# Two stacked blocks of layers: the second block's layer norms rewritten, and all layer loops written out

## The reference, cut to what matters

```
def layer_norm(x, g, b):
    mu = mean(x); var = mean(square(x - mu))      # over the 1024 features of a token
    return (x - mu) * rsqrt(var + 1e-5) * g + b

def second_block(x, p, ...):
    for i in range(2):
        proj = x @ w_in[i]                        # attention, retention, gates
        ...
        y = merged @ w_out[i]
        x = layer_norm(ALPHA * x + y, ln1_g[i], ln1_b[i])
        ffn = conv_glu_ffn(x, w_up[i], conv_w[i], conv_b[i], w_down[i])
        ple = sigmoid(x @ w_ple_gate[i]) * (p[i] @ w_ple_proj[i])
        x = layer_norm(ALPHA * x + ffn + ple, ln2_g[i], ln2_b[i])
    return x
```

## Time and profile before

| What | Value |
|---|---|
| Median of three runs | 2084.21 us (2080.54 to 2084.79) |
| Profiled execution | 2079.78 us, span 2078.0 us |
| Mean granted TensorE clock | 0.987 |
| TensorE busy | 2020.5 us, 97% |
| VectorE, ScalarE, POOL busy | 63%, 52%, 15% |

### The profile page before, as it was taken

The page is one execution under the profiler, slowest core; times in us unless marked ns, Lnnn a source line. Parts: engine busy times, 40 slices in busy tenths (PEclk is TensorE's granted clock), DMA queues, the critical chain, the costliest instruction groups (busy, mean ns, idle before and its releaser), DMA issues.

```text
span 2078.0 us, 36494 instructions
## 1 busy us (share of the span) xinstructions
PE 2020.5 (97%) x14488; PEld 1890.8 (91%) x14488; DVE 1301.7 (63%) x1504; ACT 1086.8 (52%) x1312; POOL 320.1 (15%) x239
## 2 busy tenths in 40 slices
PE   6999999999999999999999999999998999999997
PEld 5999999899889999998999999999998999998996
DVE  6555666655665576567556655577775655557775
ACT  5444565544554455655446544356655553455654
POOL 3000431300020014033003012230004203220001
PEclk9999999999999999999999999999998999999998
DMA  6554544455445545445455544554453544544551
GB/s 248 189 188 171 181 146 163 161 187 188 169 172 188 186 164 182 158 168 197 182 184 185 179 145 160 184 197 182 182 182 123 185 161 146 185 167 169 200 186 42
DMA packets 53286, 360.04 MB, mean 173 GB/s; under 512 B 6320, under 2 KB 7728, under 8 KB 10544
## 3 DMA queue, kind: packets, MB, share of 16 engines
q1 hardware_dynamic: 49248, 350.01, 46.6%
q10 hardware_dynamic: 3328, 4.20, 0.7%
q0 software_dynamic: 592, 4.19, 0.5%
HBM read 353.14 MB, written 1.05 MB: 170 GB/s over the span
## 4 chain that ended last, share of the span: by engine, by line
PE 60%; issue 30%; POOL 5%; DVE 2%; ACT 2%; DMA 1%; SPq 0%; POOLq 0%; DVEq 0%; ACTq 0%
PE up_two L1392 7%; PE gate_two L1357 7%; PE gate_two L1392 7%; PE gate_two L1358 7%; PE gate_two L1359 7%; PE bank L1357 5%; PE bank L1359 5%; PE bank L1358 5%; PE up_two L1394 4%; PE gate_two L1394 3%; POOL br_parts L404 2%; POOL in_parts L404 1%; POOL area L443 1%; PE bank L1469 1%; ACT w_hi L544 1%
## 5 line engine op out<-in xcount | busy, mean ns | idle before, releaser
L920 DVE TENSOR_TENSOR w_lo<-raw,w_hi 128x2048 fp32r<-128x2048 f32 x330 | 765.2, 2320 | 331.1 <-ACT w_hi L544 330.9
L544 ACT ACTIVATE w_hi<-raw 128x2048 fp32r<-128x2048 f32 x330 | 628.4, 1905 | 72.7 <-PE bank L1359 68.7
L1358 PE MATMUL bank<-hid_hi,w_lo 128*128 128x256 f32 x960 | 271.6, 283 | 0.0
L1357 PE MATMUL bank<-hid_lo,w_hi 128*128 128x256 f32 x960 | 271.5, 283 | 0.0
L1359 PE MATMUL bank<-hid_hi,w_hi 128*128 128x256 f32 x960 | 271.5, 283 | 0.0
L1392 PE MATMUL gate_two<-in_parts,w_hi 128*128 128x512 f32 x640 | 229.1, 400 | 4.9 <-POOL in_parts L404 4.9
L1357 PE MATMUL gate_two<-br_parts,w_hi 128*128 128x256 f32 x768 | 222.9, 290 | 9.3 <-POOL br_parts L404 8.4
L1392 PE MATMUL up_two<-in_parts,w_hi 128*128 128x512 f32 x640 | 227.8, 398 | 0.4 <-DVE w_lo L920 0.4
L1359 PE MATMUL gate_two<-br_parts,w_hi 128*128 128x256 f32 x768 | 218.8, 285 | 0.0
L1358 PE MATMUL gate_two<-br_parts,w_lo 128*128 128x256 f32 x768 | 218.7, 285 | 0.0
L1357 PEld LDWEIGHTS bank<-hid_lo,w_hi 128*128 128x128 f32 x960 | 183.7, 191 | 3.0
(11 more groups left out here) (257 smaller groups left out, 4465.4 us busy)
## 6 DMA issues: line engine op xcount, KB each, us to landing
raw<-stream SPq DMA_DIRECT2D x330, 1024.0 KB, 4.8
area<-rpb POOLq DMA_DIRECT2D x2, 1536.0 KB, 7.0
softT<-area ACTq DMA_DIRECT2D x32, 64.0 KB, 4.4
konst<-consts SPq DMA_DIRECT2D x1, 1344.0 KB, 13.2
x<-xT SPq DMA_DIRECT2D x4, 256.0 KB, 3.8
area<-area ACTq DMA_DIRECT2D x8, 128.0 KB, 5.6
ret_turn<-area ACTq DMA_DIRECT2D x8, 128.0 KB, 2.3
result<-x SPq DMA_DIRECT2D x4, 256.0 KB, 2.0
```

What stands on the lines that cost most here:

```text
L544: act.activation(w_hi[:, s, :], raw[:, s, :], ACT.Copy).then_inc(hi_ready[s], 1)
L920: dve.tensor_tensor(w_lo[:, s, :], raw[:, s, :], w_hi[:, s, :].bitcast(F32), ALU.subtract).then_inc(lo_ready[s], 1)
L1357: pe.matmul(out, whi, xlo, start=start, stop=False, skip_group_check=True)
L1358: pe.matmul(out, wlo, xhi, start=False, stop=False, skip_group_check=True)
```

## The change

In the second block:
- The variance is summed by 8 products with mean_of as the fixed operand and the squares (128x256) moving, so that it comes out the same on all 128 partitions, 128x256 in PSUM (var_ln). ScalarE adds the epsilon on the way to SBUF (rstd_ln, 128x256), and POOL raises this whole tile to -0.5. The spreading product ln_factor is gone.
- Subtraction of the mean and squares go by pairs of tiles (128x512), 4 each.
- The pair sums move from POOL to VectorE, between its additions to x.
- The lower parts move from POOL to VectorE: work + bias - br_hi, one tile behind the scaling. ScalarE first writes all upper parts and then x (in the first norm after chunk 37's work).
- The last norm makes no upper and lower parts.
- In the first norm both engines split the slot of chunk 36 ahead of their part of the norm. At the end of layer 0 the split of slot CHUNKS-3 moves into that chunk's step, and the one of CHUNKS-2 ahead of the norm on VectorE.

In both blocks the loops over layers are Python loops, so each layer has its own instructions; gains and biases are read from col1 and col2, without copies. The FFN's inner loop stays. The core of the diff:

```diff
+        rstd_ln = sb("rstd_ln", [P, T])
-        rstd_ln = banks[7][:, 1, :]
+        var_ln = banks[7][:, 0, :]
 # POOL
             def layer_norm(here, n):
-                for j in (1, 2):
-                    pool.wait_ge(z_ready.sem, here.at(z_ready, HALVES * n + j + 1))
-                    if j == 2:
-                        pool.wait_ge(z_sum.sem, here.at(z_sum, 2 * n + 1))
-                    pool.tensor_tensor(z_pairs, x[:, 0:2, :] if j == 1 else z_pairs, x[:, 2 * j:2 * j + 2, :], ALU.add
-                                       ).then_inc(z_sum.sem, 1)
                 pool.wait_ge(ln_var.sem, here.at(ln_var, n + 1))
-                power(rs[:, :], ms[:, :]).then_inc(ln_rs.sem, 1)
-                for k in range(DT):
-                    pool.wait_ge(xs_hi.sem, here.at(xs_hi, DT * n + k + 1))
-                    rest(br_lo[:, k, :], x[:, k, :], br_hi[:, k, :]).then_inc(xs_ready.sem, 1)
+                pool.tensor_tensor(rstd_ln[:, :], rstd_ln[:, :], minus_half.broadcast_to([P, T]), ALU.pow
+                                   ).then_inc(ln_rstd.sem, 1)
-            with pool.Fori(0, DEPTH) as layer:
+            for layer in range(DEPTH):
 # ScalarE
-                def layer_norm(n, col_b, spare=lambda: None):
+                def variance(n):
                     act.wait_ge(var_ready.sem, here.at(var_ready, n + 1))
-                    act.activation(ms[:, :], banks[7][:, 0, 0:TT], ACT.Identity, bias=eps5).then_inc(ln_var.sem, 1)
-                    spare()
+                    act.activation(rstd_ln[:, :], var_ln, ACT.Identity, bias=eps5).then_inc(ln_var.sem, 1)
+
+                def shifted_upper(n, col_b):
+                    for k in range(DT):
+                        act.wait_ge(ln_scaled.sem, here.at(ln_scaled, DT * n + k + 1))
+                        act.activation(br_hi[:, k, :], work[:, k, :], ACT.Identity,
+                                       bias=cur[:, col_b + k:col_b + k + 1]).then_inc(xs_hi.sem, 1)
+
+                def shifted(n, col_b):
                     for k in range(DT):
                         act.wait_ge(ln_scaled.sem, here.at(ln_scaled, DT * n + k + 1))
                         act.activation(x[:, k, :], work[:, k, :], ACT.Identity, bias=cur[:, col_b + k:col_b + k + 1]
                                        ).then_inc(x_new.sem, 1)
-                        act.activation(br_hi[:, k, :], work[:, k, :], ACT.Identity, ...
...
                     elif m == 36:
-                        layer_norm(0, C_B1, ple_first)
+                        split_after(here, m)
+                        for a in range(2):
+                            e = act.activation(ple_out[:, 2 * a:2 * a + 2, :], banks[4 + a][:, :, :], ACT.Copy)
+                        e.then_inc(mix_evac.sem, 1)
+                        variance(0)
+                        shifted_upper(0, C_B1)
                     elif m == 37:
...
                         split_after(here, m)
+                        shifted(0, C_B1)
...
                         if c == CHUNKS[1] - 3:
+                            if layer < DEPTH - 1:
+                                split_after(here, c, turn)
                             hidden_upper(here, PAIRS - 1, att_hi)
...
                 centred_squares(1)
-                layer_norm(1, C_B2)
+                variance(1)
+                if layer < DEPTH - 1:
+                    shifted_upper(1, C_B2)
+                shifted(1, C_B2)
 # VectorE
                 def centred(n):
                     dve.wait_ge(mu_ready.sem, here.at(mu_ready, n + 1))
-                    for k in range(DT):
-                        dve.tensor_tensor(x[:, k, :], x[:, k, :], banks[6][:, 0, :], ALU.subtract).then_inc(c_ready.sem, 1)
+                    mu = banks[6][:, 0:1, :].broadcast_to([P, 2, T])
+                    for j in range(HALVES):
+                        two = x[:, 2 * j:2 * j + 2, :]
+                        dve.tensor_tensor(two, two, mu, ALU.subtract).then_inc(c_ready.sem, 1)
...
+                    def shifted_lower(k):
+                        dve.wait_ge(xs_hi.sem, here.at(xs_hi, DT * n + k + 1))
+                        dve.scalar_tensor_tensor(out=br_lo[:, k, :], in0=work[:, k, :],
+                                                 scalar=cur[:, col_b + k:col_b + k + 1],
+                                                 in1=br_hi[:, k, :].bitcast(F32), op0=ALU.add, op1=ALU.subtract
+                                                 ).then_inc(xs_ready.sem, 1)
                     dve.wait_ge(ln_rstd.sem, here.at(ln_rstd, n + 1))
                     for k in range(DT):
                         dve.scalar_tensor_tensor(out=work[:, k, :], in0=x[:, k, :], scalar=cur[:, col + k:col + k + 1],
-                                                 in1=rstd_ln, op0=ALU.mult, op1=ALU.mult).then_inc(ln_scaled.sem, 1)
+                                                 in1=rstd_ln[:, :], op0=ALU.mult, op1=ALU.mult
+                                                 ).then_inc(ln_scaled.sem, 1)
+                        if lower and k >= 1:
+                            shifted_lower(k - 1)
+                    if lower:
+                        shifted_lower(DT - 1)
...
                     elif m == 36:
-                        layer_norm(0, C_G1)
                         split_after(here, m)
+                        layer_norm(0, C_G1, C_B1)
...
                 centred(1)
-                with dve.If(layer < DEPTH - 1):
-                    chunk_done(here, CHUNKS[1] - 3)
-                    split_after(here, CHUNKS[1] - 3)
-                layer_norm(1, C_G2)
-                with dve.If(layer < DEPTH - 1):
+                if layer < DEPTH - 1:
                     chunk_done(here, CHUNKS[1] - 2)
                     split_after(here, CHUNKS[1] - 2)
+                layer_norm(1, C_G2, C_B2, layer < DEPTH - 1)
 # TensorE
                 def variance(n):
                     for f in range(DT):
-                        pe.wait_ge(c_sq.sem, here.at(c_sq, DT * n + f + 1))
-                        for a in range(TT):
-                            e = pe.matmul(banks[7][:, 0, a:a + 1], work[:, f, a * P:(a + 1) * P], mean_of[:, 0:1],
-                                          start=f == 0 and a == 0, stop=f == DT - 1, skip_group_check=True)
+                        pe.wait_ge(c_sq.sem, here.at(c_sq, HALVES * n + f // 2 + 1))
+                        e = pe.matmul(var_ln, mean_of, work[:, f, :], start=f == 0, stop=f == DT - 1)
                     e.then_inc(var_ready.sem, 1)
-                def ln_factor(n):
-                    pe.wait_ge(ln_rs.sem, here.at(ln_rs, n + 1))
-                    spread_factor(rstd_ln).then_inc(ln_rstd.sem, 1)
```

More of the change, by code:

```diff
@@ L499, in _ @@
             load_tables(0, 1)
-            with pool.Fori(0, DEPTH) as layer:
+            for layer in range(DEPTH):
                 here = Place(1, layer)
+                cur = col2[:, layer, :]
                 pool.wait_ge(xs_ready.sem, here.at(xs_ready, 0))
-                pool.wait_ge(cur_ready.sem, here.at(cur_ready, 1))
+                pool.wait_ge(decay_step, 3)
                 for h in range(RET_HEADS):
@@ L532, in _ @@
                 layer_norm(here, 0)
-                with pool.If(layer < DEPTH - 1):
-                    following = nc.s_assert_within(layer + 1, 1, DEPTH - 1, skip_runtime_bounds_check_because="the If bounds it")
-                    load_tables(following, layer + 2)
+                if layer < DEPTH - 1:
+                    load_tables(layer + 1, layer + 2)
                 layer_norm(here, 1)
@@ L667, in _ @@
             act.wait_ge(small_set, SMALL)
-            with act.Fori(0, DEPTH) as layer:
+            for layer in range(DEPTH):
                 here = Place(0, layer)
+                cur = col1[:, layer, :]
                 split_hi(2, here.uses(2))
@@ L754, in _ @@
                 ffn(here, FFN_CHUNKS + MIX1, 1)
-                norm_input(here, 3, gain1, range(HALVES))
+                norm_input(here, 3, gain1(layer + 1), range(HALVES))
             act.wait_ge(col2_in, 16)
@@ L901, in step @@
                         hidden_upper(here, i + 1)
[L902 to L906, removed]
+                    if c == CHUNKS[1] - 3:
+                        pass
+                    elif c == CHUNKS[1] - 2:
+                        if layer < DEPTH - 1:
+                            chunk_done(here, c, turn)
                             split_after(here, c, turn)
@@ L1075, in _ @@
                 dve.sem_inc(x_ready.sem, 1)
-                xg_lower(Place(0, 0), 0, gain1, [j])
+                xg_lower(Place(0, 0), 0, gain1(0), [j])
             for s in range(2):
                 split_lo(s, 0)
-            with dve.Fori(0, DEPTH) as layer:
+            for layer in range(DEPTH):
                 here = Place(0, layer)
-                dve.tensor_copy(cur[:, 0:COLS1], col1[:, bass.ds(layer, 1), :].rearrange("p a c -> p (a c)")
-                                ).then_inc(cur_ready.sem, 1)
```

(11 more changed lines are left out.)

58 lines of the change are left out of this document (30 added, 28 removed).

## The result

The changed kernel takes 2225.92 us (median of 4 runs, 2221.74 to 2229.66) against 2083.05 us for the kernel before beside it: a ratio of 1.0686 (1.0658 to 1.0715), slower by 143 us. The profiled execution took 2221.74 us.

A forecast was written before the change was run, and what follows sets the result against it. TensorE, busy 97% of the span, was taken as the bound, so exposed waits count. Norm terms 73.8 + 35.6 + 34.8 gave +144.2 us on 2079.78, 2224.0; with 4.4 us to the median, 2228 us, range 2108 to 2262.

The forecast's parts named there:

- The price of the power: POOL's 256-column power in each of four norms: 0.40 us fixed plus 0.155 us a column, 40.1 us.
- a cheaper loop: POOL's wide power: 5 to 36 us if partly unrolled, 2084 to 2212 (chance 0.09); below 5 us if cheap, 2068.6 (0.19).
- a dearer one: Rival on POOL's wide power: 46.6 us each, 26 us more in all, 2254 us; chance 0.03.
- the blocked form: POOL's 2-column power of 2.67 us in the kernel before: it waited for a VectorE split and took 0.58 us itself.
- the free ones: POOL's undisturbed powers in the kernel before: 2 columns 0.71 us, 8 columns 1.64 us, which gave the slope.
- some 35 us: Sign of being right: TensorE waits this long before chunk 38 and before layer 1 for VectorE's br_parts.
- The norms: Four layer norms of the second block: first norms +36.9 us each, second of layer 0 +35.6, last +34.8.
- 6.3 were reckoned: Last norm: time from the power's end at 2106.5 to the span's end at 2112.8.
- Writing the loops out: Layer loops: removes seven small copies and their waits; put at zero, bounds -2 to +2 us.
- POOL's freed time: About 8 us a norm on POOL, claimed to go to nothing that anyone waits for.
- If a long power holds VectorE's work in turn: Possible port exclusion during POOL's power in the norms: what counts is VectorE's queue; costed at nothing.

The follow-up runs named there:

- e6_widths: Kernel before, with unread POOL powers of 4 to 256 columns and one 256-column addition added in each layer's first FFN of the first block: 2081.09 us, ratio 0.9990.
- e3_half: Changed kernel with the power of only the first 128 columns, the rest of the factor constant 0.5: 2145.42 us, ratio 1.0312.
- e5_loops: Kernel before with only the layer loops written out in all engines, copies of gains and biases kept: 2076.50 us, ratio 0.9974.
- e1_columns: Changed kernel with only the power put back: variance as columns, POOL's 2-column power, spread by TensorE; other edits kept: 2069.38 us, ratio 0.9934.

## Why the prediction was right

**The price of the power.** This step carried the forecast, and it held at 32 times the width: 40.1 us worked out from 2 and 8 columns, 41.24 measured. The error of 1.1 us, four times, is 4.6 us of the sum. Telling the blocked form from the free ones was needed: with 2.67 us for 2 columns no slope comes out. The rivals of a cheaper loop and of a dearer one both fall by e6_widths.

**All of it is exposed.** e3_half shows 80.5 us for 82 in the medians and 20.4 to 20.6 us a norm for 20.4 in the traces. The waits themselves are 40.9 to 43.5 us, more than the "some 35 us" that the forecast named as a sign; the price of a norm is less than its wait, as TensorE also waited before, 1.99 us in the first norm and 3.47 in the second.

**The norms.** With the power at 41.2 in place of 40.1 the forecast would read +38.0, +36.7, +38.0 and +35.9. Measured are +39.0, +35.6, +37.7 and +35.3. All are within what one trace can tell, but two causes are seen in the rows. In the first TensorE waits 0.82 us for the mask addition. In the second and the last the sum of squares took 3.72 us, where the narrow products before had taken 5.00 and 5.36; the clock granted in the stretch of the 5.00 us was 0.72, and in that of the new sum 1.00. In the last norm the end came 6.75 us after the power where 6.3 were reckoned, which takes 0.45 back. While the power of the second norm runs the clock does fall, but the new sum stands ahead of it. The window inside that power (busy us of PE, PEld, DVE, ACT and POOL, then the granted clock, the DMA share and GB/s):

```profile
1620.00:1662.00 42.00, 0.00 (x0) 0.00 (x0) 0.37 (x1) 0.38 (x1) 41.14 (x1) 0.53 0.07 25
```

No engine but POOL works, but for 0.4 us of VectorE and ScalarE at the ends, and the grant is 0.53, close to the 1.2 GHz level (0.50 from 1630 on); the first products after it are 0.21 us apart, as reckoned.

**The small edits.** Writing the loops out was put at zero with bounds of -2 to +2; with the copies gone it gives -5.7 us, outside them (-5.0 for the loops alone in e5_loops). The step that failed reads "TensorE is not waiting for them at a layer's start", which looked at the copies and took one wait of 2.1 us as all that the boundary costs; the first products after it also ran at a lower clock (a grant of 0.70 in 570.3 to 576 before, 1.00 in e5_loops).

That POOL's freed time "goes to nothing that anyone waits for" was wrong. It brings load_tables forward, and its addition, which had held VectorE where nobody waited, now holds it where TensorE waits. With the long power this cost 0.8 us, as the power itself delays POOL; in e1_columns TensorE stands 5.68 us for it, and cutting the addition gave 4.6 us in the medians.

"If a long power holds VectorE's work in turn" turned out not to be so. The Trainium skill, "SBUF — State Buffer", section "SBUF: two separate sides", has the port pair that VectorE and GpSimd share, which VectorE needs for an operation with two SBUF inputs, held for the whole instruction by whichever starts first. For the plain addition the trace agrees (6.67 us for a lower part of 0.48), apart from the first moments: a lower part that began 0.06 us behind the addition still took 0.48 us. For the power it doesn't: VectorE's splits, which also read two tiles of SBUF, kept 2.29 us all through 41.12 us of it, and here the measurement decides.

The errors of -5.7 (loops), +4.6 (power) and about -1 (norms) leave the sum 2.3 us off. The power's price and its exposure were right by their mechanism; that the total came so near is in part luck, as the first two errors cancel.

## What to carry to other kernels

Find the price of a column on POOL from two undisturbed widths of the same operation before widening it; a power there costs 0.16 us a column (128 elements) where an addition costs about 2.4 ns (0.61 us for 256), so raise statistics as columns and spread them. When work leaves an engine, look at what stands next in its queue: it starts earlier and may fall on the chain. A long plain POOL operation beside work of VectorE that TensorE waits for is better cut into pieces, as VectorE gets in between.

## What the runs showed of the hardware that I had not expected

- A POOL power of 41.12 us leaves VectorE's two-input operations at their 2.29 us, while a POOL addition of 7.1 us stretches one of 0.48 us to 6.67, and eight pieces of it stretch none by more than 0.8 us.
- The price of the power is a straight line from 2 to 256 columns, 0.159 us each with 0.3 us fixed.
- A hardware loop's passage from one layer to the next costs TensorE 3.5 us in the first block and nothing measurable in the second; why they differ is open. With the loops ScalarE also made 21 loads of its function tables in place of 18.
